# Up projection of a two-layer float32 block: the third and fourth chunk of every quarter computed as a pair with seven products for eight

## The reference

```python
hn = rmsnorm(x, norm_ffn_pre[l])
u = jnp.square(jax.nn.relu(jnp.einsum('bsd,df->bsf', hn, w_up[l])))
y = jnp.einsum('bsf,fd->bsd', u, w_down[l])
x = x + rmsnorm(y, norm_ffn_post[l])
```

## Time and profile before

| | us |
|---|---|
| median of 3 runs | 2559.22 |
| lowest, highest | 2558.97, 2559.31 |
| profiled execution | 2559.44 |
| its span (first to last instruction) | 2557.7 |
| PE busy | 2551.5 (100%) |
| DVE busy | 1764.6 (69%) |
| ACT busy | 1296.9 (51%) |
| POOL busy | 34.8 (1%) |

### The profile page before, as it was taken

The page is one execution under the profiler, slowest core; times in us unless marked ns, Lnnn a source line. Parts: engine busy times, 40 slices in busy tenths (PEclk is TensorE's granted clock), DMA queues, the critical chain, the costliest instruction groups (busy, mean ns, idle before and its releaser), DMA issues.

```text
span 2557.7 us, 29454 instructions
## 1 busy us (share of the span) xinstructions
PE 2551.5 (100%) x11425; PEld 2115.1 (83%) x11425; DVE 1764.6 (69%) x2062; ACT 1296.9 (51%) x1554; POOL 34.8 (1%) x56
## 2 busy tenths in 40 slices
PE   9999999999999999999999999999999999999999
PEld 7888888888888888888888888888888888888887
DVE  5646565566666666776876777678678768778686
ACT  6554443444555555455454544445465455455463
POOL 1000000000000000000000000000020000000000
PEclk9999999999999999999999999999999999999999
DMA  8767766676776777778566787666757677666674
GB/s 271 216 189 210 205 202 196 190 208 204 215 220 196 215 196 200 219 227 230 165 181 181 206 223 201 203 206 198 244 174 223 195 216 212 215 196 224 204 231 141
DMA packets 534795, 527.42 MB, mean 206 GB/s; under 512 B 294896, under 2 KB 297824, under 8 KB 534656
## 3 DMA queue, kind: packets, MB, share of 16 engines
q1 hardware_dynamic: 531856, 518.09, 68.3%
q0 software_dynamic: 2384, 6.93, 1.1%
q10 hardware_dynamic: 416, 0.52, 0.1%
HBM read 488.24 MB, written 2.10 MB: 192 GB/s over the span
## 4 chain that ended last, share of the span: by engine, by line
PE 100%; ACT 0%; DVE 0%; issue 0%; ACTq 0%
PE bank L2312 30%; PE bank L2313 30%; PE bank L2314 30%; PE bank L2379 2%; PE bank L2380 2%; PE bank L2381 2%; PE bank L2498 1%; PE bank L2487 1%; PE bank L2477 1%; PE bank L2411 0%; PE bank L2420 0%; PE bank L2433 0%; PE bank L2426 0%; PE bank L2558 0%; PE bank L2545 0%; PE bank L2578 0%
## 5 line engine op out<-in xcount | busy, mean ns | idle before, releaser
L1255 DVE TENSOR_TENSOR t_wl<-t_stage,t_wh 128x1024 fp32r<-128x1024 f32 x844 | 1021.4, 1220 | 600.2 <-ACT t_wh L714 594.8
L714 ACT ACTIVATE t_wh<-t_stage 128x1024 fp32r<-128x1024 f32 x845 | 885.1, 1057 | 801.4 <-PE bank L2314 758.3
L2312 PE MATMUL bank<-t_wl,t_xth 128*128 128x512 f32 x2400 | 941.0, 392 | 0.5 <-DVE t_xtl L1297 0.5
L2314 PE MATMUL bank<-t_wh,t_xtl 128*128 128x512 f32 x2400 | 934.1, 389 | 0.0
L2313 PE MATMUL bank<-t_wh,t_xth 128*128 128x512 f32 x2400 | 934.0, 389 | 0.0
L2314 PEld LDWEIGHTS bank<-t_wh,t_xtl 128*128 128x128 f32 x2400 | 450.5, 188 | 94.1
L2312 PEld LDWEIGHTS bank<-t_wl,t_xth 128*128 128x128 f32 x2400 | 450.6, 188 | 93.9 <-DVE t_xtl L1297 0.9
L2313 PEld LDWEIGHTS bank<-t_wh,t_xth 128*128 128x128 f32 x2400 | 450.7, 188 | 92.5 <-issue 0.2
L2312 PE MATMUL bank<-t_wl,t_yth 128*128 128x512 f32 x914 | 355.6, 389 | 0.0
L2313 PE MATMUL bank<-t_wh,t_yth 128*128 128x512 f32 x914 | 355.1, 389 | 0.0
L2314 PE MATMUL bank<-t_wh,t_ytl 128*128 128x512 f32 x914 | 355.1, 389 | 0.0
(11 more groups left out here) (410 smaller groups left out, 1509.4 us busy)
## 6 DMA issues: line engine op xcount, KB each, us to landing
t_stage<-in_a_w_in_dram SPq DMA_DIRECT2D x192, 512.0 KB, 4.3
t_stage<-in_w_in_dram SPq DMA_DIRECT2D x168, 512.0 KB, 4.3
t_stage<-in_b_w_in_dram SPq DMA_DIRECT2D x128, 512.0 KB, 4.5
t_stage<-in_w_up_dram SPq DMA_DIRECT2D x92, 512.0 KB, 4.4
t_stage<-in_w_down_dram SPq DMA_DIRECT2D x90, 512.0 KB, 5.1
t_stage<-in_a_w_out_dram SPq DMA_DIRECT2D x64, 512.0 KB, 4.3
t_ubuf<-in_w_down_dram SPq DMA_DIRECT2D x38, 512.0 KB, 5.3
t_ubuf<-in_w_up_dram SPq DMA_DIRECT2D x36, 512.0 KB, 4.5
```

The source lines that it names most:

```text
L714: e.activation(wh[:, j % N_SPLIT], stage[s], ACT.Copy).then_inc(*hi(j))
L1255: e.tensor_tensor(low, src, high.bitcast(F32), ALU.subtract).then_inc(*lo(j))
L2312: e.matmul(o, h, w_l, start=start, stop=False)
L2314: return e.matmul(o, l, w_h, start=False, stop=stop)
```

## The change

Four pairs are added, (up,q,2)/(up,q,3) for q of 0 to 3. The list of groups grows to 965: per pair 12 plain groups and 7 products stand where 16 plain groups stood, and PE has 42 matmuls for the four first k-tiles where it had 48. The list of products lies so that P1, P5, P6 and P7 of (up,q,2)/(up,q,3) come between the last groups of (up,q,0)/(up,q,1), and those of (down,q,0)/(down,q,1) between the last groups of the new pair. `apart`, `together`, `up_sum` and `sums` are written for the new pairs too; `apart` waits for the transposition of (up,q,0) and `together` for that of (up,q,1), whose buffers they overwrite. `low_after` gives new places for up_low and up_high, and the sums of x3 are made earlier, in (up,0,1) instead of (up,0,2). POOL's row for the last norm waits for a product of (up,3,2) instead of (up,3,0).

```diff
-            [((kind, q, c), (kind, q, c + 1)) for q in range(4) for kind, c in (("up", 0), ("down", 0), ("down", 2))
+            [((kind, q, c), (kind, q, c + 1)) for q in range(4) for kind in ("up", "down") for c in (0, 2)
...
-        if ("up", q, c) in pair_of:
-            return 8 if c == 0 else 10
-        return 8 if c == 3 else 4
+        behind = 4 if q == 0 and c < 2 else (6, 10, 4, 8)[c]
+        return behind + end("up", q, c if q == 0 and c < 2 else c | 1) - end("up", q, c)
...
         e.wait_ge(*vec.at("sF"))
+        def squared(q, c):
+
+            t = buf[c % 2]
+            slot(end("up", q, c))
+            if ("up", q, c) in pair_of:
+                e.wait_ge(*vec.at("sum", "up", q, c))
+            else:
+                e.wait_ge(*used.at(end("up", q, c) - 1))
+            for i in range(2):
+                e.activation(t[:, i, :], t[:, i, :] if ("up", q, c) in pair_of else accs("up", q, c)[i],
+                             ACT.Relu, scale=sF[:, i:i + 1]).then_inc(*act("up", q, c, i))
+            e.wait_ge(*act.at("up", q, c, 1))
+            e.activation(t, t, ACT.Square).then_inc(*act("squared", q, c))
+
         for q in range(4):
...
+            squared(q, 0)
+            if q == 0:
+                slot(end("up", 0, 0) + 3)
+                sum_high("x3")
+                up_high(0, 0)
+            squared(q, 1)
+            apart(first_of["up", q, 2], turned.at("up", q, 0))
+            if q:
+                up_high(q, 0)
+            up_high(q, 1)
+            squared(q, 2)
+            squared(q, 3)
+            apart(first_of["down", q, 0], vec.at("late", first_of["down", q - 1, 2], 1) if q >= 2 else None)
+            up_high(q, 2)
             up_high(q, 3)
...
         for q in range(4):
-            if ("up", q, 0) in pair_of:
+            if q:
                 for c in range(2):
                     up_sum(q, c)
                     up_turn(q, c)
+            else:
+                up_turn(0, 0)
+                slot(end("up", 0, 0) + 2)
+                split_sums(xth, xtl, rowb.rearrange("p a b -> p (a b)"), vreg[:, 7168:8192], "x3")
+                slot(end("up", 0, 0) + 3)
+                sum_low("x3")
+                up_low(0, 0)
+                up_turn(0, 1)
+            slot(end("up", q, 1) + 2)
+            together(first_of["up", q, 2], turned.at("up", q, 1))
+            if q:
                 up_low(q, 0)
...
+            up_low(q, 1)
+            for c in (2, 3):
+                up_sum(q, c)
+                up_turn(q, c)
             if q:
                 late(first_of["down", q, 0])
             else:
                 together(first_of["down", q, 0])
```

More of the change, by code:

```diff
@@ L695, in gpsimd @@
         for c in range(4):
-            e.wait_ge(*(vec.at("dr", c - 2, 1) if c >= 2 else used.at(where[first_of["up", 3, 0], P3])))
+            e.wait_ge(*(vec.at("dr", c - 2, 1) if c >= 2 else used.at(where[first_of["up", 3, 2], P3])))
             load_row(c, A["norm_ffn_post_2"][:, cols(c)], "ffn", c)
@@ L1178, in scalar @@
         e.wait_ge(*vec.at("sF"))
-        for q in range(4):
-            for c in range(4):
-                if (q, c) == (0, 2):
-                    slot(end("up", 0, 1) + 2)
-                    sum_high("x3")
-                early_turn = ("up", q, 1) in pair_of
-                if c == 3 and early_turn:
-                    up_high(q, 1)
-                if c and not (c == 1 and early_turn):
-                    up_high(q, 0 if c == 2 and early_turn else c - 1)
-                if c == 3:
-                    m = first_of["down", q, 0]
-                    apart(m, vec.at("late", m - 2, 1) if q >= 2 else None)
-                slot(end("up", q, c))
-                halved_ = ("up", q, c) in pair_of
-                if halved_:
-                    e.wait_ge(*vec.at("sum", "up", q, c))
-                else:
-                    e.wait_ge(*used.at(end("up", q, c) - 1))
-                    if (q, c) >= (0, 2):
-                        e.wait_ge(*turned.at("up", *((q, c - 2) if c >= 2 else (q - 1, c + 2))))
-                for i in range(2):
-                    e.activation(buf[c % 2][:, i, :], buf[c % 2][:, i, :] if halved_ else accs("up", q, c)[i],
-                                 ACT.Relu, scale=sF[:, i:i + 1]).then_inc(*act("up", q, c, i))
-                e.wait_ge(*act.at("up", q, c, 1))
-                e.activation(buf[c % 2], buf[c % 2], ACT.Square).then_inc(*act("squared", q, c))
@@ L1205, in scalar @@
             up_high(q, 3)
-            if ("down", q, 2) in first_of:
-                m = first_of["down", q, 2]
-                apart(m, vec.at("late", m - 1, 1) if q else None)
-            if ("up", q + 1, 0) in first_of:
+            if q < 3:
+                apart(first_of["down", q, 2], vec.at("late", first_of["down", q, 0], 1) if q else None)
                 apart(first_of["up", q + 1, 0], turned.at("up", q, 2))
@@ L2164, in vector @@
                 together(first_of["down", q, 0])
-            up_turn(q, 3)
+            up_low(q, 2)
             up_low(q, 3)
```

13 lines of the change are left out of this document (removed).

## The result

The changed kernel takes 2619.3 us (median of 4 runs, 2618.23 to 2620.41) where the kernel before takes 2559.26 on the same chip: ratio 1.0235, interval 1.0217 to 1.0253. It is 60.0 us slower; 50.1 were forecast, with 2610 as the likeliest time and 2594 to 2626 as the range. The profiled execution took 2618.23, its span is 2616.5.

The account below looks back on a forecast made before the run. PE was taken as the bound, held where pairs meet by late DVE and ACT steps: 7.2 + 5.75 + 3 x (5.5 + 8.7) = 55.6 us, less 5.44, +50.1 on 2559.44, 2609.5, with a few tenths 2610; range 2594 to 2626.

Parts of the forecast that it names:

- The bound and the price of a matmul: PE bounds the kernel; a matmul costs 0.227 us from start to start, so 24 fewer save 5.44 us.
- The walk: Step-by-step timing of DVE, ACT and PE where pairs meet, giving 55.6 us of new PE waits.
- second place: Where (up,q,2) ends as the next pair begins: 8.7 us in quarters 1 to 3, 5.75 in quarter 0.
- U: Time zero of the timing: end of group (up,q,0) 14, or of (up,q,2) 14 at a second place.
- first places: Where (up,q,0)/(up,q,1) end as the new pair begins: 5.5 us in quarters 1 to 3, 7.2 in quarter 0.
- DVE's start: DVE not quite free when a second place begins, low parts 0.1 to 0.6 late, three times: a few tenths.
- Lowest for a place: only the second sum: Lower bound: PE held only by the second sum, 1.4 us; eight such are 11 us, less 5.44: 2565.
- all three holds: PE's waits for the second sum and late low parts; claimed not to add up, the last holding them all.
- Elsewhere nothing moves: Outside those places no cost: down projection keeps its order, ACT has no long row, loads lead by over 14 us.
- the clock: Rival, chance 0.14: 5 us idle before P4 halves PE's clock, up to 2 us at three second places: 2616.
- about 15 us longer: Expected sign by stage: each of quarters 1 to 3 about 15 us longer, quarter 0 12.

Follow-up runs that it names:

- the last kernel: Against the preceding rearranged kernel (pairs kept, holds worked on), quarter 0's first transposition two groups later, its send behind four loads: 2554.05 us, ratio 0.9978.
- The kernel with filled waits: The changed kernel with matmuls that nobody reads added in all of PE's long waits: 2611.81 us, ratio 1.0204.

## Why the prediction was right, and where it was off

*The bound and the price of a matmul.* Right, and shown by the last kernel: with the holds of this part gone, 24 matmuls less are worth 5.5 us for 5.44 forecast.

*The walk, step by step.* At the second place of quarter 1 every step of DVE lies 0.4 to 0.5 behind the forecast and none has another distance: the sum at U+0.4 for 0.03, low part U+5.2 for 4.75, second sum U+12.8 for 12.36, transposition U+19.2 for 18.71, low part of P4 U+26.7 for 26.19. The kernel with filled waits puts the first places at 5.7 for 5.5, quarter 0 at 7.3 and 5.9 for 7.2 and 5.75, the second places at 9.2 for 8.7. The mis-sized term is DVE's start: it is not free when a second place begins, as its low parts there end 0.5 us after U. I had counted a few tenths for all three places together; it was 0.5 for each.

*"Lowest for a place: only the second sum."* Not reached; in the trace all three holds bite one after another (1.92, 0.76, 5.58 us), and the last absorbs the others, as the walk said.

*Elsewhere nothing moves.* Right. No load held PE in the changed kernel. (The lead of five groups that I gave there as over 14 us is 13.6 by my own 2.72 a group.)

*The step that failed* is the clock, the case I gave 0.14 and 2616 us and left out of the sum of the forecast. Two things were wrong in it. I took 3.7 idle us at the end of the trace at a granted 1.00 as evidence that a wait of 5 us may pass; the drop came in each of the three second places that wait 5 us or more. And the drop isn't bound to the longest waits: three of six drops stand behind others, two of them behind waits of 2 us. Filled waits, and nothing else, gave 6.4 to 7.8 us back. That my price for the case, 6 us, was near is in part luck: the three places for which I had reckoned 2 us each cost 4.8 together, and 1.6 came from quarter 2's first place, which I had not counted. The Trainium skill (TensorE: Matmul & The Clock Gate, Part 1) says that idleness halves PE's clock and activity releases it; the rows of the changed kernel agree with both halves (0.51 from 2162 to 2169, behind the wait, and 1.00 from 2169 to 2176, while PE took its matmuls without one).

*A sign that contradicts the sum.* I wrote that quarters 1 to 3 would be "about 15 us longer" each. The sum says 5.5 + 8.7 - 1.36 = 12.8, and only that gives 50.1. Measured were 15.0, 16.9 and 15.0; that 15 came true is luck.

*Sum by terms.* 55.6 forecast, 2.3 for DVE's late start and smaller remainders, 6.4 for half clock: 64.3; less 5.44 that is 58.9, and 58.8 between the spans. The remaining 1.2 of the 60.0 lies between medians and profiled executions.

*Open.* Which wait of 2 us brings the low clock and which doesn't, and why. The same wait at the same place had it in quarter 2 and not in quarters 1 and 3 of the changed kernel, and in all three with late moved. No run here was made to settle that.
